# Part of the merge's first gate tile moved into attention, and the merge's token block sums moved to the pool engine

## What is computed

```python
(gq, gk, gv, lq, lk, lv, lr, lgo, dq, dk, dv, merge) = split_columns(h @ p['w_in'][l])
...
outs = jnp.stack([gqa_out, gla_out, diff_out], axis=2)
y = jnp.einsum('bnie,ied->bnid', outs, p['w_branch'][l])
gates = jax.nn.sigmoid(merge.reshape(b, n, N_BRANCH, D_MODEL))
mixed = jnp.sum(gates * y, axis=2) @ p['w_out'][l]
```

## Time and profile before

| | us |
|---|---|
| median of 3 runs | 2432.31 |
| lowest and highest | 2431.68, 2436.39 |
| the profiled execution, its own time | 2432.91 |
| its span, first to last instruction | 2431.1 |

### The profile page before, as it was taken

The page is one execution under the profiler, slowest core; times in us unless marked ns, Lnnn a source line. Parts: engine busy times, 40 slices in busy tenths (PEclk is TensorE's granted clock), DMA queues, the critical chain, the costliest instruction groups (busy, mean ns, idle before and its releaser), DMA issues. The chain is left out here.

```text
span 2431.1 us, 40928 instructions
## 1 busy us (share of the span) xinstructions
PE 2338.4 (96%) x16479; PEld 2169.0 (89%) x16479; DVE 1497.9 (62%) x2400; ACT 1073.7 (44%) x2129; POOL 215.9 (9%) x176
## 2 busy tenths in 40 slices
PE   7989989899999999999999899898999999999999
PEld 6867867699999899999998688677999989999998
DVE  5335567776665874756753546686676568567473
ACT  5533446744442542533345233675444335335252
POOL 1421000100003100000134110000000040000000
PEclk8989999999999999999999999999999999999999
DMA  9244133032235122332231531301222432323122
GB/s 274 70 144 151 54 114 124 8 96 79 79 113 156 49 91 70 87 98 60 87 96 53 166 130 41 102 1 61 65 81 74 147 114 70 100 57 105 55 81 83
DMA packets 246698, 224.03 MB, mean 92 GB/s; under 512 B 6976, under 2 KB 232336, under 8 KB 246000
## 3 DMA queue, kind: packets, MB, share of 16 engines
q1 hardware_dynamic: 242240, 218.59, 28.7%
q10 hardware_dynamic: 3760, 2.17, 0.4%
q0 software_dynamic: 512, 0.66, 0.3%
HBM read 211.70 MB, written 9.70 MB: 91 GB/s over the span
## 5 line engine op out<-in xcount | busy, mean ns | idle before, releaser
L2289 ACT ACTIVATE ring_high<-raw 128x512 fp32r<-128x512 f32 (+1 forms) x278 | 158.1, 609 | 252.1 <-PE ps L2648 146.4
L2433 DVE TENSOR_TENSOR ring_low<-raw,ring_high 128x512 fp32r<-128x512 f32 (+1 forms) x278 | 204.8, 762 | 74.8 <-ACT ring_high L2289 70.7
L2721 PE MATMUL ps<-hH,ring_low 128*128 128x320 f32 x640 | 197.9, 309 | 0.3
L2721 PE MATMUL ps<-hL,ring_high 128*128 128x320 f32 x640 | 197.8, 309 | 0.0
L2721 PE MATMUL ps<-hH,ring_high 128*128 128x320 f32 x640 | 197.7, 309 | 0.0
L1497 DVE SCALAR_TENSOR_TENSOR xT<-ps,mod,xT 128x512 f32<-128x512 f32 (+1 forms) x128 | 64.0, 545 | 188.8 <-PE ps L2648 188.8
L359 PE MATMUL ps<-wH,hL 128*128 128x512 f32 (+1 forms) x460 | 173.8, 378 | 2.6 <-DVEq L1053 1.4
L359 PE MATMUL ps<-wH,hH 128*128 128x512 f32 (+1 forms) x460 | 171.0, 372 | 0.0
L2648 PE MATMUL ps<-gH,ring_low 128*128 128x320 f32 x704 | 160.9, 310 | 0.3 <-DVE xT L1497 0.3
L2648 PE MATMUL ps<-gH,ring_high 128*128 128x320 f32 x704 | 160.4, 309 | 0.0
L2648 PE MATMUL ps<-gL,ring_high 128*128 128x320 f32 x704 | 160.3, 309 | 0.0
(11 more groups left out here) (384 smaller groups left out, 6275.9 us busy)
## 6 DMA issues: line engine op xcount, KB each, us to landing
raw<-in_w_in SPq DMA_DIRECT2D x56, 1024.0 KB, 5.2
raw<-in_w_ffn_in SPq DMA_DIRECT2D x88, 512.0 KB, 5.1
gmod<-in_w_mod SPq DMA_DIRECT2D x16, 1024.0 KB, 6.4
modw<-in_w_mod SPq DMA_DIRECT2D x16, 1024.0 KB, 5.5
raw<-in_w_ffn_out SPq DMA_DIRECT2D x16, 1024.0 KB, 5.4
b_raw<-in_w_branch SPq DMA_DIRECT2D x22, 512.0 KB, 3.9
head_w<-in_w_mod SPq DMA_DIRECT2D x8, 1024.0 KB, 13.2
raw<-in_w_out SPq DMA_DIRECT2D x8, 1024.0 KB, 6.1
```

What stands on the lines that cost most here:

```text
L2289: nc.scalar.activation(ring_block(m.ring_high, b, src.shape[1], src.shape[2]), src, ACT.Copy).then_inc(m.sem("w_high"), 1)
L2433: nc.vector.tensor_tensor(ring_block(m.ring_low, b, nk, cols), src, ring_block(m.ring_high, b, nk, cols).bitcast(F32), ALU.subtract).then_ ...
L2721: last = nc.tensor.matmul(m.ps[:, plan.banks[n, 0][BANK[what]], 0:HALF], w[:, k, :], a[:, k, :], start=(first and k == 0 and q == 0), stop ...
```

## The change

Three edits.

1. The tile (0, 0) is computed in attention: k = 0 to 2 at the end of round S - 1, k = 3 and 4 at the end of round S, k = 5 to 7 at the end of round S + 1, into PSUM banks 0 and 1. The merge starts with tile (0, 1), and `tile_done` is raised by 1 at once.
2. `next_high` and `next_low` run in rounds 28 and 30 in both layers.
3. The ten 128x1280 operations of the block sums are issued by GpSimd at the start of the merge's block, in the same order, without a wait before the first. `t_low` on VectorE waits for `t_summed` too, as it writes over the sums.

```diff
+    GATE_PART = {S - 1: range(0, 3), S: range(3, 5), S + 1: range(5, KT)}
...
+                if i in GATE_PART:
+                    if i == S - 1:
+                        pe.wait_ge(m.sem("next_low"), 1)
+                        pe.wait_ge(m.sem("exp_done"), 2 * (S - 2) + 2)
+                    transposed_tile(nc, m, 0, 0, W256, KT, m.hH, m.hL, 0, 0, GATE_PART[i])
...
-                if i == (35 if more else 28):
+                if i == 28:
                     next_high(nc, m, act, nxt)
...
-                if i == (36 if more else 30):
+                if i == 30:
                     next_low(nc.vector, m, dve, nxt)
...
+        @block.gpsimd
+        def _(pool):
...
+            def difference(to, spare, x, y):
+
+                a = order.step(nc.gpsimd.tensor_tensor(to, x[0], y[0], ALU.subtract))
+                b = order.step(nc.gpsimd.tensor_tensor(spare, x[1], y[1], ALU.subtract))
+                pool.wait_ge(*a)
+                pool.wait_ge(*b)
+                nc.gpsimd.tensor_tensor(to, to, spare, ALU.add).then_inc(m.sem("t_summed"), 1)
+
+            def less(to, x, t):
+
+                a = order.step(nc.gpsimd.tensor_tensor(to, x[0], t, ALU.subtract))
+                pool.wait_ge(*a)
+                nc.gpsimd.tensor_tensor(to, to, x[1], ALU.add).then_inc(m.sem("t_summed"), 1)
+
+            difference(m.gt_sum[0][:, :, :], m.gt_spare[0][:, :, :], h12, h11)
+            difference(m.gt_sum[2][:, :, :], m.gt_spare[2][:, :, :], h22, h12)
+            pool.wait_ge(m.sem("t_summed"), 1)
+            less(m.gt_sum[1][:, :, :], h22, m.gt_sum[0][:, :, :])
+            pool.wait_ge(m.sem("t_summed"), 3)
+            less(m.gt4[:, :, :], h21, m.gt_sum[1][:, :, :])
...
             def t_low(i):
                 t = (0, 2, 1)[i]
                 dve.wait_ge(m.sem("t_high"), i + 1)
+                dve.wait_ge(m.sem("t_summed"), (3, 3, 4)[i])
...
+            pe.sem_inc(m.sem("tile_done"), 1)
             for g in plan.gates:
                 if g < PLAIN_GATES:
                     for c in range(2):
+                        if (g, c) == (0, 0):
+                            continue
```

More of the change, by code:

```diff
@@ L3027, in _ @@
             mix_high((6, 7))
+        @block.gpsimd
+        def _(pool):
+            order = Signal(m.sem("pool_order"))
+            h11, h12 = ([x[:, 0:4, c * HALF:(c + 1) * HALF] for x in (m.hH.bitcast(F32), m.hL.bitcast(F32))] for c in range(2))
+            h21, h22 = ([x[:, 4:8, c * HALF:(c + 1) * HALF] for x in (m.hH.bitcast(F32), m.hL.bitcast(F32))] for c in range(2))
+            def difference(to, spare, x, y):
[14 more added lines that the diff above has]
+            less(m.gt4[:, :, :], h21, m.gt_sum[1][:, :, :])
         @block.vector
@@ L3080, in turned_low @@
                 ins.then_inc(m.sem("turned_low"), 1)
[L3082 to L3097, removed]
             def t_low(i):
@@ L3130, in _ @@
             done = order.step(nc.vector.reciprocal(m.sml[:, 40:60], m.sml[:, 20:40]))
-            difference(m.gt_sum[0][:, :, :], m.gt_spare[0][:, :, :], h12, h11)
-            difference(m.gt_sum[2][:, :, :], m.gt_spare[2][:, :, :], h22, h12)
             for g in plan.gates:
@@ L3164, in _ @@
                         mix_low(range(6))
[L3165 to L3170, removed]
+                    if g == 1 and what == 0:
                         t_low(0)
```

## The result

The changed kernel takes **2462.2 us** (median of 4 runs, 2460.3 to 2465.1), the kernel before 2433.0 beside it on the same chip: ratio 1.0117, 95% interval 1.0105 to 1.0129. It is slower by 29 us, 25.5 to 31.4 by the interval. Forecast were 2458 and a range of 2441 to 2470.

What follows compares the result with a forecast made beforehand. TensorE, busy 96% of the span, was taken as the bound. Late merge starts (5.1, 4.0 us) plus 8.2 a layer gave 25.5, taking 2432.91 to 2458.4; the median, 0.6 lower, about 2458, range 2441 to 2470.

Steps and rivals of the forecast that it cites:

- The taking of turns: Merge's start: VectorE and GpSimd alternate whole operations, 3.47 us a turn, block 5 done at 21.0 not 6.54; chance 0.62.
- The chain behind it: Merge, after block 5: gate load at 21.1 us, data at 26.3, sigmoid at 29.5, delaying tile (1, 0); +8.2 us a layer.
- The lower clock: Merge, around tile (1, 0): a gap before it makes 1.6 us more likely; its end taken as 38.0 us.
- Attention: Attention's end: the tile's matmuls and the earlier weight split start the merge late, +5.1 us first layer, +4.0 second.
- Edit 3's saving on VectorE: Merge: VectorE loses ten operations of 1.49 us a layer, worth nothing since TensorE waited for none of them.
- The sum: Both layers: 13.3 us in the first and 12.2 in the second, together 25.5 us slower, to 2458 us.

Runs made afterwards that it cites:

- split_sums: Changed kernel with each of GpSimd's ten 128x1280 operations issued as two of 128x640; 2442.3 us, ratio 1.0038 to the kernel before.
- write_sums: Changed kernel with each of GpSimd's ten operations replaced by three memsets of the same target, block sums left out; 2427.4 us, ratio 0.9976 to the kernel before.
- tile_only: Kernel before with edits 1 and 2 alone, the block sums staying on VectorE; 2437.4 us, ratio 1.0017 to the kernel before.
- vector_gap: Edits 1 and 2, sums on VectorE, the first of two differences moved between blocks 5 and 6; 2428.4 us, ratio 0.9973 to the kernel before.

## Why the prediction was right

**The taking of turns** was the step that decided, and it held in every number: a turn of 3.47 us at 640 columns was worked out, (504.85 - 494.51) / 3 = 3.45 measured; block 5 at 21.0, measured 20.6 (GpSimd began with TensorE and not 0.35 behind it); GpSimd's operation 2.92 us, measured 2.88 to 2.97. It was read off for 640 columns; split_sums and write_sums show the two things those rows could not, that the hold goes with the whole instruction and that operations which read hold, while memsets do not.

**The chain behind it.** Forecast: (1, 0) starts at 29.5 or 30.4, by the sigmoid or by block 6. Measured 30.4 by the sigmoid in the first layer, 30.1 by block 6 in the second. The first is 0.9 late: the load went out 0.5 earlier than forecast, but took 6.56 us from issue to use and not 5.20; why is open. The lower clock was put at 1 us a layer; it came to 2.3 in one and to nothing in the other, after gaps of 3.8 and 3.6 us (the stretch behind each):

```profile
519.48:526.31 6.83, 4.98 (x19) 4.98 (x20) 6.83 (x7) 4.98 (x8) 4.11 (x2) 0.50 0.20 63
1722.83:1729.66 6.83, 6.83 (x47) 6.83 (x48) 6.83 (x8) 2.39 (x5) 2.68 (x1) 1.00 0.18 30
```

**Attention.** Forecast +5.1 and +4.0, measured +4.2 and +4.6. The three k put behind the last values cost little: in the second layer these values begin 3.69 us ahead of the merge and not 2.87, though 2.6 us of matmuls stand between. TensorE's gap went from 3.43 and 2.19 to 0.45 in both layers, a little less than the 0.69 I had taken from another barrier. The rest of the price is what was put ahead of the last values. That the forecast meets each layer within 1 us is partly luck: the second layer's +4.6 was +3.3 to +5.1 in the six other profiles of the same attention.

**Edit 3's saving on VectorE** was put at nothing. With edit 1 in place that is too low: tile_only shows that the old place of the sums costs 4.5 us a layer once TensorE is early, and then freeing VectorE is worth as much (222.4 us from (1, 0) to `out` in write_sums, 226.8 in tile_only). It did not enter the time, as TensorE came to (1, 0) 7.7 and 7.4 us later than before. The same hole is in my expectation for tile_only.

**The sum.** 25.5 forecast, 26.2 in the two stretches, 27.4 in the span, 29.2 between the medians, with an interval that reaches from 25.5 to 31.4. That the first two are so close is partly luck: the four parts missed by -0.9, +0.6, +1.8 and -0.8 us, which nearly cancel. Of the rest, 1.2 us lie outside the two stretches, and 1.8 come from which execution was profiled: 2460.3 is the lowest of the four.

## What to carry to other kernels

Before work moves to GpSimd to relieve VectorE, look what VectorE issues beside it. If GpSimd reads SBUF and VectorE has two inputs there, each of its operations waits for a whole operation of GpSimd; short operations of VectorE on the way to a DMA then pay many times their own length, and long operations on GpSimd make it worse. An engine's own idle time, here 6 us of VectorE behind the gate load, was the better place. And when TensorE is made to arrive earlier, list what was ready just in time before: 7.4 us of head start turned into three new waits.

## What the hardware showed beside this

- The clock makes a profile's total differ where the code does not. From `out` of the first layer to the second attention all kernels run the same program; in ten profiles it took 797.6 to 803.6 us. In tile_only, at 803.6, the granted clock was 0.50 from 1354.82 to 1361.65. The wait of 2.78 us that ends there stands in every kernel; in vector_gap it is 2.79 long and the clock stays full behind it:

```profile
1355.29 0.55 PE L763 MATMUL ps<-lv,g_am 128*128 128x128 f32 x1 [2.78 <-DVE g_s L840]
...
1354.82:1361.65 6.83, 6.36 (x72) 5.64 (x72) 1.39 (x3) 0.69 (x4) 0.00 (x0) 0.50 0.27 91
...
1353.51 0.35 PE L763 MATMUL ps<-lv,g_am 128*128 128x128 f32 x1 [2.79 <-DVE g_s L840]
...
1353.04:1359.87 6.83, 6.36 (x120) 5.25 (x124) 4.04 (x10) 0.69 (x4) 0.00 (x0) 1.00 0.30 97
```

  That is why the stretches, and not the totals, are compared above; a wait of 2.8 us can be followed by either level, and by itself it does not tell which.
- Two gaps of nearly one length in the changed kernel (3.77 and 3.60 us, each behind a wait of 10 us and two branch tiles) ended differently: the clock was lower behind the first and full behind the second. The time of such a gap can only be given as a range.
- GpSimd writes 128x1280 in 1.2 us (a memset) and takes 2.9 for a subtraction of that size.
